# Reading: pairing the projection units of HGRN heads 2 to 7, with one more step of the head's own work moved on VectorE and ScalarE

## What is computed

```python
proj = h @ w_in
q, f, i, g = jnp.split(proj, 4, axis=-1)
log_f = jnp.logaddexp(jnp.log(lb), jnp.log1p(-lb) + jax.nn.log_sigmoid(ff))
k = (1.0 - lb) * jax.nn.sigmoid(-ff)
qf = jax.nn.silu(q.astype(jnp.float32)) * (HGRN_HEAD_DIM ** -0.5)
o = _hgrn2_chunk_scan(heads(qf), heads(k), heads(i.astype(jnp.float32)), heads(log_f))
o = o * lax.rsqrt(jnp.mean(o * o, axis=-1, keepdims=True) + NORM_EPS)
```

## Time and profile before

| what | value |
|---|---|
| median of 3 runs | 2268.04 us (2267.93 to 2269.16) |
| the profiled execution, its own time | 2269.89 us |
| its span | 2268.1 us |
| granted TensorE clock, mean | 0.999 |
| PE busy | 2255.4 us, 99% of the span |
| DVE, ACT, POOL busy | 72%, 40%, 53% |
| stage touched by the change | about 44 to 377 us (iterations 1 to 7) |

### The profile page before, as it was taken

The page is one execution under the profiler, slowest core; times in us unless marked ns, Lnnn a source line. Parts: engine busy times, 40 slices in busy tenths (PEclk is TensorE's granted clock), DMA queues, the critical chain, the costliest instruction groups (busy, mean ns, idle before and its releaser), DMA issues.

```text
span 2268.1 us, 32503 instructions
## 1 busy us (share of the span) xinstructions
PE 2255.4 (99%) x10798; PEld 1886.9 (83%) x10798; DVE 1639.1 (72%) x2304; ACT 898.2 (40%) x1467; POOL 1202.4 (53%) x1357
## 2 busy tenths in 40 slices
PE   9999999999999999999999999999999999999998
PEld 7888888888888888888888888888888888888887
DVE  7666666856778778776666777666787787787766
ACT  5233333324535434443432224322453454344433
POOL 4332323234566566656546665764556665666562
PEclk9999999999999999999999999999999999999999
DMA  4101110124264555455313211112335545554553
GB/s 158 38 29 38 29 37 28 38 75 148 93 210 147 181 185 200 140 195 187 112 56 113 73 38 38 56 56 93 130 131 186 208 143 185 185 190 146 198 197 140
DMA packets 59722, 273.82 MB, mean 121 GB/s; under 512 B 7152, under 2 KB 10352, under 8 KB 41712
## 3 DMA queue, kind: packets, MB, share of 16 engines
q1 hardware_dynamic: 58512, 269.99, 34.8%
q10 hardware_dynamic: 1120, 2.65, 0.3%
HBM read 210.75 MB, written 61.87 MB: 120 GB/s over the span
## 4 chain that ended last, share of the span: by engine, by line
PE 93%; DVE 3%; DVEq 1%; POOL 1%; ACT 1%; DMA 1%; issue 0%; SPq 0%; POOLq 0%; ACTq 0%
PE prod_ps L955 10%; PE prod_ps L957 10%; PE prod_ps L956 10%; PE prod_ps L1221 8%; PE prod_ps L1223 8%; PE prod_ps L1222 8%; PE side_ps L1221 7%; PE side_ps L1223 7%; PE side_ps L1222 7%; PE side_ps L1096 2%; PE side_ps L1008 2%; PE prod_ps L1647 2%; PE prod_ps L1649 2%; PE prod_ps L1648 2%; PE prod_ps L1635 2%; PE prod_ps L1637 2%
## 5 line engine op out<-in xcount | busy, mean ns | idle before, releaser
L955 PE MATMUL prod_ps<-operand_hi,w_hi 128*128 128x512 f32 x984 | 393.0, 399 | 2.5 <-DVE operand_lo L1824 1.6
L957 PE MATMUL prod_ps<-operand_hi,w_lo 128*128 128x512 f32 x984 | 384.5, 391 | 0.0
L956 PE MATMUL prod_ps<-operand_lo,w_hi 128*128 128x512 f32 x984 | 383.5, 390 | 0.0
L706 POOL CAST w_hi<-w_raw 128x1024 fp32r<-128x1024 f32 x59 | 64.8, 1099 | 467.0 <-PE prod_ps L957 409.4
L751 POOL TENSOR_TENSOR w_lo<-w_raw,w_hi 128x256 fp32r<-128x256 f32 x168 | 155.4, 944 | 128.3 <-ACT w_hi L3045 127.6
L710 POOL TENSOR_TENSOR w_lo<-w_raw,w_hi 128x256 fp32r<-128x256 f32 x236 | 216.7, 948 | 4.7
L955 PEld LDWEIGHTS prod_ps<-operand_hi,w_hi 128*128 128x128 f32 x984 | 185.1, 188 | 39.8 <-DVE operand_lo L1824 2.1
L957 PEld LDWEIGHTS prod_ps<-operand_hi,w_lo 128*128 128x128 f32 x984 | 184.8, 188 | 40.1
L956 PEld LDWEIGHTS prod_ps<-operand_lo,w_hi 128*128 128x128 f32 x984 | 185.2, 188 | 35.7
L751 POOL TENSOR_TENSOR w_lo<-w_s,w_hi 128x256 fp32r<-128x256 f32 x168 | 129.1, 772 | 141.9 <-ACT w_more_hi L3053 116.5
L2256 DVE TENSOR_TENSOR x_res<-prod_ps,x_res 128x512 f32<-128x512 f32 x130 | 89.0, 684 | 95.0 <-PE prod_ps L1223 95.0
(11 more groups left out here) (450 smaller groups left out, 6336.8 us busy)
## 6 DMA issues: line engine op xcount, KB each, us to landing
w_raw<-stream SPq DMA_DIRECT2D x202, 512.0 KB, 3.7
x_park<-x_res SPq DMA_DIRECT2D x45, 1024.0 KB, 8.3
x_res<-x_park SPq DMA_DIRECT2D x45, 1024.0 KB, 6.8
swapped<-op_park SPq DMA_DIRECT2D x39, 1024.0 KB, 5.1
op_park<-swapped SPq DMA_DIRECT2D x6, 1024.0 KB, 7.9
x_in<-x_t SPq DMA_DIRECT2D x16, 256.0 KB, 5.6
x_res<-x_t SPq DMA_DIRECT2D x8, 512.0 KB, 4.6
end_park<-x_res SPq DMA_DIRECT2D x4, 1024.0 KB, 4.3
```

What stands on the lines that cost most here:

```text
L955: nc.tensor.matmul(into, w_h, a_h, start=(k == 0), stop=False)
L956: nc.tensor.matmul(into, w_h, a_l, start=False, stop=False)
L957: last = nc.tensor.matmul(into, w_l, a_h, start=False, stop=(k == KT - 1))
```

## The change

Units 6 to 23 (heads 2 to 7) become nine pairs. `paired` and its helpers now take a description of the stage (`PairedStage`), so that one code serves both mixers. The tile `x_in` is laid out in another order, so that the sums T1 to T4 of the activation blocks, which are made in iteration 1 from `x_in` (`in1_combine`, `in1_low`), find room; the block of tiles 0 and 1, tokens 512 to 1023, is overwritten by T4 and loaded again at the end of the stage (`x_12`, `high_12`, `low_12`). Two heads make three pairs, and the steps are put at the eight places within each pair.

The lower bound goes from DVE to ACT: an Identity activation with scale and bias replaces the multiplication of the decay on DVE, and the factor of the key goes into the product of query and sigmoid (line 1989 becomes two SCALAR_TENSOR_TENSOR instructions of 256 columns). Iterations 2 to 7 copy the scores of levels 1 to 6 first, and then grow. The loop over iterations 4 to 7 is written out.

```diff
+            def hgrn_steps(n, par):
...
+                elif n % 2 == 0:
+                    mids = [turn_v_and_last_level, turn_k, chunk_kv, None, lambda: newer_level(4), lambda: newer_level(5)]
+                    ends = [lambda: newer_level(0), lambda: newer_level(1), lambda: newer_level(2), third_level_then_out,
+                            None, sixth_level_then_back]
+                else:
+                    mids = [None, lambda: newer_level(0), kv_then_second_level, lambda: newer_level(3), None, None]
+                    ends = [turn_v_and_last_level, keys_then_first_level, None, out_then_fourth_level,
+                            lambda: newer_level(5), sixth_level_then_back]
...
+            def two_heads(n):
+
+                steps = [hgrn_steps(n + k, k) for k in range(2)]
+                mids, ends = steps[0][0] + steps[1][0], steps[0][1] + steps[1][1]
+                for p in range(3):
+                    m0, m1, m2, m3 = mids[4 * p:4 * p + 4]
+                    e0, e1, e2, e3 = ends[4 * p:4 * p + 4]
+                    paired(in1, (3 * n - U_PAIRED1) // 2 + p,
+                           {"P2": m0, "c11": e0, "P6": m1, "c12": e1, "P7": m2, "c22": e2, "P4": m3, "c21": e3})
...
+                part(1)
+                free(n_u)
+                seventh(b_u, A11, B11, True).then_inc(s.prod, 1)
+                part(3)
+                free(n_v)
+                sum_ready(1)
+                seventh(b_v, S1, T1, True).then_inc(s.prod, 1)
+                free(n_w)
+                seventh(b_w, A12, B21, True)
+                then("P2")
+                part(4)
+                plain(b_w, 0, 0, False).then_inc(s.prod, 1)
+                then("c11")
+                copied(1)
+                part(5)
+                sum_ready(2)
+                seventh(b_u, S2, T2, False).then_inc(s.prod, 1)
+                then("P6")
+                free(n_z)
+                plain(b_z, 0, 1, True)
+                part(6)
...
-                    grow(b, number)
+                    scores_first = 1 <= number <= LEVELS - 2 and 2 <= n < HEADS1
+                    if not scores_first:
+                        grow(b, number)
...
+                    if scores_first:
+                        grow(b, number)
                     dve.drain()
...
+                if 2 <= n < HEADS1:
+                    level(par, LEVELS - 1)
+                    group(0)
+                    newer_level(0)
+                    if par:
+                        group(1)
+                        newer_level(1)
+                    else:
+                        first_pair_of(u)
+                        newer_level(1)
+                        group(1)
+                    states()
+                    newer_level(2)
+                    group(2)
+                    newer_level(3)
+                    if par:
+                        first_pair_of(u + 1)
+                    group(3)
+                    newer_level(4)
...
+                nc.scalar.activation(f, f, ACT.Sigmoid, scale=-1.0)
+                act.drain()
+                nc.scalar.activation(kept, kept, ACT.Identity, bias=lb[:, 3, n:n + 1], scale=lb[:, 4, n:n + 1]
+                                     ).then_inc(gates, 1)
...
+            def odd_iteration(n, j):
+                take_v(n)
+                q_sigmoid(n - 1, 1)
+                in_high_more(in1, j)
+                newer_gather(n, 1)
```

More of the change, by code:

```diff
@@ L31 @@
 from contextlib import ExitStack
+from dataclasses import dataclass
 import numpy as np
@@ L1999, in third, with states @@
                         gate_low(h, j % 2, 16 + 2 * h + j % 2 + 1)
[L2001 to L2014 removed]
+                def states():
+                    step = hgrn_step(n, "kv")
                     kv = done_step(step).rearrange("p (c v) -> p c v", c=NB)
@@ L2973, in _, with q_sigmoid @@
-            for n in range(4):
-                hgrn_iteration(n, n % 2)
-            with act.Fori(2, HEADS1 // 2) as i:
-                hgrn_iteration(i * 2, 0, i=i)
-                hgrn_iteration(i * 2 + 1, 1, i=i)
+            def q_sigmoid(n, part):
+                q, par = 3 * n + 2, n % 2
+                half = halves_of(q)[part]
+                act.wait_ge(*written(q, half))
+                nc.scalar.activation(by_chunk(sig[:, half]), h_part(par, True, half), ACT.Sigmoid).then_inc(q_sig, 1)
```

931 lines of the change are left out of this document (568 added, 363 removed).

## The result

The changed kernel takes 2280.52 us (median of 6 runs, 2279.89 to 2284.05) against 2268.2 us (6 runs, 2267.9 to 2269.16) for the kernel before: ratio 1.0055, 95% interval 1.0043 to 1.0068. It is slower by some 12 us. I had forecast 2271.8 with a range of 2262 to 2280; the time lies just above it. The profiled execution took 2279.89 us with a span of 2278.1 us.

What follows compares the result with a forecast made beforehand. PE was taken to bound the kernel, busy 99% of the span at clock 1.00. Waits of 16.3 us less 12.5 saved made 3.8 us, added to the median 2268.04: 2271.8 us, range 2262 to 2280.

Steps and rivals of the forecast that it cites:

- Waits 11.7 + 2.0 + 0.5 + 2.1 = 16.3, saved 12.5: Whole change: new PE waits of 16.3 us against 12.5 us of matmuls left out, so 3.8 us longer.
- L3 of odd iterations: PE waits 1.5 us for the gather, behind kv, states, two score copies and growth.
- even ones: L3 in even iterations: PE arrives after 11.6 us, the gather after 12.6, so PE waits 1.0 us.
- L0 odd: L0 in odd iterations: query product late behind ACT's `take_v` and last q sigmoid; PE waits 0.55 us (0.4 to 0.95).
- L1 odd: L1 in odd iterations: DVE gets L0's scores out after 6.1 us, PE arrives after 5.3; PE waits 0.85 us.
- L5 in iteration 1: Once, gather stands behind the second f sigmoids and a high part on ACT; PE waits 2.0 us (1 to 2.8).
- unit 24: Once, POOL splits it only after the last pair's A22, in 4.6 us; PE waits some 0.5 us (0 to 1).
- two readers: DVE instructions with two SBUF inputs slow beside POOL: 0.7 us per two heads, 2.1 in all (0 to 6).
- The second rival: POOL and DVE in each other's way on the chains, L6 joining: stalls 22 to 25 us, time 2277 to 2280; chance 0.2.
- the mark I had set: Two L0 steps an iteration pair apart on PE: over 99 us would mean POOL and DVE hinder each other; 96.8 to 97.5 expected.
- Twenty-four matmuls take 5.57 us, 0.232 us each.: PE's matmul pace; the 54 matmuls that nine pairs leave out are worth 12.5 us.
- The other edits cost nothing.: Lower bound on ACT lies in ACT's gaps, no chain ends where DVE is relieved; written-out loop changes no order: 0 us.

Runs made afterwards that it cites:

- the second: Changed kernel with the gather for L5 in iteration 1 put ahead of the second f sigmoids and T3's high part on ACT: 2276.12 us, ratio 1.0036 to before.
- the third experiment: Changed kernel with POOL splitting unit 24 once the last pair's product with S2 is done, not after A22: 2278.66 us, ratio 1.0045 to before.
- the five edits: Changed kernel with growth first, L5's gather first, unit 24 split early, L0 ahead of v evacuation, q sigmoid ahead of v: 2265.53 us, ratio 0.9987 to before.
- the fifth experiment: Changed kernel with the last q sigmoid of the head before put ahead of the copy of v on ACT in odd iterations: 2279.72 us, ratio 1.0051 to before.
- the first experiment: Changed kernel with the growth ahead of the score copies again in iterations 2 to 7: 2275.76 us, ratio 1.0031 to before.
- The fourth experiment: Changed kernel with DVE doing L0's growth and scores ahead of the v projection's first half in odd iterations: 2278.21 us, ratio 1.0035 to before.

## Why the prediction was wrong

**The step that failed: the sum takes a wait at its idle time.** "Waits 11.7 + 2.0 + 0.5 + 2.1 = 16.3, saved 12.5" puts nothing on top. The runs showed two things in its place.

First the clock, 1.7 us behind L5 and 1.7 behind unit 24, 3.4 in all. The way from L5 to L6 of iteration 1 takes 5.37 us in the changed kernel (the first two rows) and 3.66 in the kernel before (the third, by L5 at 78.41 of the earlier trace rows):

```profile
80.35 1.68 PE L1189 MATMUL side_ps<-hgrn_kq,hgrn_mixed 128*128 128x128 f32 x8 [2.29 <-ACT hgrn_mixed L3165]
85.72 1.06 PE L1189 MATMUL side_ps<-hgrn_kq,hgrn_mixed 128*128 128x128 f32 x8
82.07 1.05 PE L1096 MATMUL side_ps<-hgrn_kq,hgrn_mixed 128*128 128x128 f32 x8
```

That the wait brings the fall rests on three runs: the low clock went with the wait in the second and in the third experiment, and came with the one idle that was put into the kernel before. The same wait does not bring it every time (last section).

Second, a delay has edges that no view of waits lists. Per two heads (L0 of iterations 4 and 6) the steps on PE take 30.2 us beside the listed waits, 29.3 in the kernel before: 0.9. Levels that waited take 0.9 to 1.0 us for 0.81. The product matmul ahead of L0 and of both L3 counts 0.39 us up to the idle and not 0.23: 0.5. That is 1.4 us for two heads. It does not go with the listed waits: with the five edits PE's busy time is the same, and rows at L3 and L6 are still long by up to 0.25 us where the view lists nothing. A step that comes just in time pays the edge too.

**The waits.** Here it held in mechanism for the most part. Forecast 16.3 us, measured 16.95: L3 of odd iterations 1.12 (forecast 1.5), of even ones 0.70 to 0.95 (1.0), L0 odd 0.72 (0.55), L1 odd 1.54 (0.85), L5 in iteration 1 2.29 (2.0), unit 24 1.85 and 0.32 ahead of `back` (0.5). That the totals agree to 0.65 us is in part luck: L1 and unit 24 together are 3.7 us above their forecast, L3 is 1.8 below, and the 2.1 for two readers had no place of its own. Two terms were mis-sized. At L1, I took L7's growth at 1.14 and its decay at 0.24; in the changed kernel they are 1.57 and 0.69, both beside POOL, which is 0.9 us, and the wait is 0.7 longer than I said. At unit 24, "a split is 13.80 / 3 = 4.6 us": it takes 6.6, as DVE works beside it,

```profile
380.18 1.83 POOL L797 CAST w_hi<-w_raw 128x1024 fp32r<-128x1024 f32 x1 [28.39 <-PE prod_ps L1330]
382.09 4.76 POOL L801 TENSOR_TENSOR w_lo<-w_raw,w_hi 128x256 fp32r<-128x256 f32 x4
```

and the wait comes out at 1.85. I had written that I would be wrong if PE waited for a weight part; it did.

**"L0, odd iterations."** The size was near, the reason was not: not the sigmoid behind `take_v`, but DVE, as the fifth experiment shows.

**"Two readers of SBUF."** Forecast 2.1 us in all; the experiments give 0.5 us per two heads with POOL lightened and 0.4 at L1, some 2.7 in all. The second rival, of which this was the core, is not what happened, though the time is near its 2277 to 2280: the view lists no wait at L6, and the mark I had set (over 99 us for two heads) was missed twice, with 98.6 and 98.2, and met only where unit 24's wait lies in the stretch.

**"Twenty-four matmuls take 5.57 us, 0.232 us each."** This was sound. Inside a run of products starts are 0.229 us apart and the first behind a step takes 0.32; summed over two heads, the products take 67.8 us before and 63.9 after, 3.9 saved, and 4.4 without the three long matmuls ahead of waits. So 12.5 us was a little low (13.1 by these rows) for what left PE, and the edges took it back.

**The ledger.** In the stage the sum was 16.3 - 12.5 = 3.8 us and the traces have 12.2. The 8.4 between them are 0.65 for the waits and 3.4 for the clock; the rest, 4.3, is what remains when PE's own work at full clock falls by 8.2 us (333.19 to 325.0) and not by 12.5: 13.1 of matmuls less 4.9 of edges. Of these the pairs' 1.4 us per two heads make 4.1; the rest I have not placed. Between the forecast and the median there are 8.7 us, and the last 0.3 are not in the stage.

**"The other edits cost nothing."** Wrong for both named parts. The lower bound on ACT costs nothing but is worth 13.7 us against the one other place that was tried: there the change is slower by 26. I had said that no chain ends in the second half of an iteration. One does, that of `back`. And "copying first has its return at places where a step waits for the half": it has none; it costs 1.1 to 1.4 us per two heads in the changed kernel, and 0.7 us an iteration even in the kernel before. My L3 chains did have the copies in them; I did not ask what the other order gives.

## What to carry to other kernels

Removing matmuls from a PE that is 99% busy pays only as far as the chains beside it keep up: here 13 us of matmuls went into fifteen waits, their edges and two falls of the clock, and it took five reorderings of a line or two to end 2.9 us below the kernel before. Price a delayed step at its listed idle time plus some 0.3 us of edges, also where it comes just in time, and where the idle is near 2 us, at up to nearly double, for the clock that may fall behind it. When a step is moved ahead of another on an engine without gaps, ask at every one of its places who waits for the one behind.

## What the runs showed of the hardware

In the traces of all these kernels together PE had 19 idle stretches of 1.8 to 2.6 us between 40 and 420 us. Behind 14 of them the granted clock fell (to between 0.57 and 0.78 in the lowest stretch of 4 us), behind 5 it did not, with the same kernel and the same idle: the 2.29 us of iteration 1 brought the fall in four of the six kernels that have it unchanged and not in the other two. Behind none of the shorter waits of the stage, up to 1.57 us, did it fall; but at the norm step ahead of it a wait of 1.1 to 1.2 us, in five of the traces, was followed by a fall in two (0.76 and 0.84 in 40 to 44 us) and by none in three. I had no term for any of it; which idle brings the fall stays open. In iteration 1 of the first experiment, the clock did not fall behind L5; PE then came to L0 of iteration 2 2.3 us too early, waited 2.31 us there, and the clock fell after that (0.57 in 100 to 104 us). The fourth experiment has the same. Two long waits hid one another: without the fall behind L5, L0 of iteration 2 came 48.38 us after L0 of iteration 1, with it 47.61.

A DVE growth of 1024 columns with both inputs in SBUF takes 1.21 to 1.26 us in the changed kernel when no subtraction of POOL runs beside it or when it starts first, and 1.32 to 1.79 when POOL's subtraction has started before it.
